# Gate/up of a pair ahead of the down product of the pair before it, in a two-layer decoder kernel with 64 experts

## What is computed

```python
def swiglu(x, wg, wu, wd):
    return (jax.nn.silu(x @ wg) * (x @ wu)) @ wd
top_idx, top_w = route(xf, w_router, router_bias)      # 8 of 64 experts for a token
y = routed_experts(xf, top_idx, top_w, w_gate, w_up, w_down) + swiglu(xf, ws_gate, ws_up, ws_down)
```

## Time and profile before

| | |
|---|---|
| median of 3 runs | 1187.65 us (1187.37 to 1188.17) |
| the profiled execution | 1188.19 us, its span 1186.4 us |
| mean granted clock of TensorE | 0.996 |
| PE busy | 1148.7 us (97%) |
| PEld, DVE, ACT busy | 523.0, 352.7, 255.3 us |
| HBM read, written | 452.22 MB, 3.15 MB; mean of all traffic 385 GB/s |
| the chain that ended last | PE 76%, DMA 21%, DVE 2% |

### The profile page before, as it was taken

The page is one execution under the profiler, slowest core; times in us unless marked ns, Lnnn a source line. Parts: engine busy times, 40 slices in busy tenths (PEclk is TensorE's granted clock), DMA queues, the critical chain, the costliest instruction groups (busy, mean ns, idle before and its releaser), DMA issues.

```text
span 1186.4 us, 15935 instructions
## 1 busy us (share of the span) xinstructions
PE 1148.7 (97%) x6752; PEld 523.0 (44%) x6752; DVE 352.7 (30%) x1053; ACT 255.3 (22%) x511; POOL 8.4 (1%) x20
## 2 busy tenths in 40 slices
PE   8999999999999999999999999999999999999995
PEld 7774633433343333333386655333343334333331
DVE  0424722222222222222333346232222222222224
ACT  1132421222122211111112323221222122112111
POOL 0000000000000000000000000000000000000001
PEclk9999999999999999999999999999999999999998
DMA  9982599999999999999998626999999999999995
GB/s 378 421 328 113 213 415 425 428 427 426 428 426 427 428 427 428 427 427 428 413 425 360 252 80 254 412 428 428 426 429 426 428 427 426 429 426 428 426 425 224
DMA packets 39952, 456.49 MB, mean 385 GB/s; under 512 B 4416, under 2 KB 4544, under 8 KB 8256
## 3 DMA queue, kind: packets, MB, share of 16 engines
q1 hardware_dynamic: 39872, 455.38, 91.5%
HBM read 452.22 MB, written 3.15 MB: 384 GB/s over the span
## 4 chain that ended last, share of the span: by engine, by line
PE 76%; DMA 21%; DVE 2%; issue 0%; ACT 0%; POOL 0%; POOLq 0%; DVEq 0%
PE bank L705 29%; DMA slots<-in_w_gu 20%; PE bank L725 14%; PE bank L926 5%; PE bank L854 5%; PE bank L607 4%; PE bank L634 4%; PE bank L863 2%; PE bank L1052 2%; PE bank L825 1%; PE bank L713 1%; PE bank L829 1%; PE bank L873 1%; PE bank L883 1%; PE bank L959 1%; PE bank L619 1%
## 5 line engine op out<-in xcount | busy, mean ns | idle before, releaser
L705 PE MATMUL bank<-slots,front 128*64 128x512 f32 x2048 | 456.0, 595 | 13.6 <-DMA slots<-in_w_gu 13.5
L705 PEld LDWEIGHTS bank<-slots,front 128*64 128x64 f32 x2048 | 139.9, 137 | 280.8 <-issue 249.4
L725 PE MATMUL bank<-slots,r 128*32 128x512 f32 x2016 | 229.9, 595 | 1.1 <-issue 1.1
L1403 DVE SCALAR_TENSOR_TENSOR yparts<-bank,small,yparts 128x512 fp32r<-128x512 f32 x128 | 96.0, 750 | 265.4 <-ACT yparts L1086 265.4
L1086 ACT ACTIVATE yparts<-bank,small 128x512 fp32r<-128x512 f32 x128 | 87.9, 687 | 239.8 <-PE bank L725 239.8
L1395 DVE TENSOR_TENSOR high<-high,bank 128x256 f32<-128x256 f32 x64 | 26.9, 421 | 354.5 <-ACT high L1113 326.7
L725 PEld LDWEIGHTS bank<-slots,r 128*32 128x32 f32 x2016 | 59.3, 109 | 137.2 <-issue 135.7
L1113 ACT ACTIVATE high<-bank 128x256 f32<-128x256 f32 x60 | 23.0, 384 | 413.1 <-PE bank L705 413.1
L1086 ACT ACTIVATE front<-bank 128x512 f32<-128x512 f32 (+1 forms) x161 | 84.5, 580 | 88.7 <-PE bank L825 28.2
L607 PEld LDWEIGHTS bank<-selr,xparts 128*128 128x128 f32 x512 | 64.3, 188 | 45.4 <-issue 45.4
L634 PE MATMUL bank<-yparts 64*128 64x512 f32 x512 | 79.4, 421 | 1.9 <-DVE yparts L1403 1.9
(11 more groups left out here) (123 smaller groups left out, 616.6 us busy)
## 6 DMA issues: line engine op xcount, KB each, us to landing
slots<-in_w_gu SPq DMA_DIRECT2D x116, 2048.0 KB, 30.8
slots<-in_w_dn SPq DMA_DIRECT2D x58, 2048.0 KB, 27.5
slots<-in_dense SPq DMA_DIRECT2D x28, 1024.0 KB, 14.8
slots<-in_w_gu SPq DMA_DIRECT2D x24, 1024.0 KB, 9.0
slots<-in_w_dn SPq DMA_DIRECT2D x10, 1024.0 KB, 37.4
slots<-in_first SPq DMA_DIRECT2D x3, 768.0 KB, 7.0
r<-in_pool_mat SPq DMA_DIRECT2D x2, 1024.0 KB, 25.9
sdn<-in_shared_dn SPq DMA_DIRECT2D x2, 1024.0 KB, 10.0
```

The source lines that it names most:

```text
L705: m = pe.matmul(H[64 * a:64 * a + 64, :], cells[:, cell(B, k, j), a, :], GU[g][:, a, :, k, :], start=k == 0, stop=k == KD - 1)
L725: m = pe.matmul(Y[half][r0:r0 + 32, :], hT[:, kc * P + 64 * a + 32 * t:kc * P + 64 * a + 32 * t + 32], wd[:, a, kc, :], start=kc == 0, sto ...
L1403: dve.scalar_tensor_tensor(ysp[:, 1, half * 512:(half + 1) * 512], Y[half][:, :], wslot[:, b:b + 1], ysp[:, 0, half * 512:(half + 1) * 512 ...
```

## The change

The first matmul group of body q is unchanged; what follows is reordered on all engines, in the main pass and in the spare passes (which run only if an expert has more than 32 tokens):

- PE, body q > 0: gate/up(q), both halves of down(q-1) (`down_both`), turn(q), gather, combine(q-1) half 0, gather, combine(q-1) half 1, turn_sel(q+1). Body 0 has no down. The body now covers all 32 pairs; pair 31's down comes behind the loop, with combine(30) half 1 between its halves, as before. At a block's first pair gate/up starts with six of eight gathers evacuated and waits for the others at k = 6 and 7.
- ACT: silu(q), both `hi` of q-1, then the two gathers' evacuations. DVE: `gated(q)`, `lo(q-1)` half 0, `turned(q)`, `lo(q-1)` half 1, `take_selT(q+1)`.
- SP: body q issues gate/up of q, then down of q-1.
- Pair 2's second gate/up half is loaded as two quarters. The first waits only for the first half of the shared expert's last product (`sgu_rd`) and is issued ahead of the load into `xs`, the second for `sh1` as before, behind it.

```diff
@@ SP
+                def give_dn(q):
+                    sp.wait_ge(ps.y_full, 2 * (base + q - 2))
...
+                        load_dn(ps, l, q, q % 3)
...
-                    sp.wait_ge(ps.y_full, 2 * (n - 2))
-                    load_dn(ps, l, q, g)
+                    if q > 3:
+                        give_dn(q - 1)
...
-                sp.wait_ge(*full_at(l, "sh1"))
-                load_gu(main, l, 2, 2, (1,))
+                a, m, z = W_CHUNK, W_CHUNK + W_CHUNK // 2, 2 * W_CHUNK
+                sp.wait_ge(sgu_rd, l + 1)
+                sp.dma_start(slots[:, 2, a:m], w_gu[l * PAIRS + 2][:, a:m]).then_inc(third_in, 16)
...
+                sp.wait_ge(*full_at(l, "sh1"))
+                sp.dma_start(slots[:, 2, m:z], w_gu[l * PAIRS + 2][:, m:z]).then_inc(main.w_in[1][2], 16)
@@ PE, body
                     gate_up(n, q, g, use, first)
+                    if first:
+                        refill(0)
+                        refill(1)
+                        if round_ is None:
+                            shared_turn(l, 1)
+                        turn_h(n)
+                    else:
+                        down_both(n - 1, q - 1, (q - 1) % 3, (q - 1) // 3)
+                        turn_h(n)
+                        begins = l if q == 1 and round_ is None else None
+                        if filling:
+                            refill(0)
+                        combine(ps, n - 1, 1 - b, 0, begins)
+                        if filling:
+                            refill(1)
+                        if not last:
+                            combine(ps, n - 1, 1 - b, 1, begins)
@@ PE, down_both
+                    pe.wait_ge(ps.hT_sb, n + 1)
...
+                        if B + 1 < BLOCKS:
+                            pe.wait_ge(ps.g_sb, first_fill + KD * (B + 1) + 2 * j + half + 1)
+                        else:
                             pe.wait_ge(ps.lo_rd, 2 * n - 1 + half)
                         down(q, g, half)
+                        if half == 0 and q == PAIRS - 1:
+                            combine(ps, n - 1, 0, 1)
@@ ACT, body
+                    if not first:
+                        hi(n - 1, 1 - b)
+                    if B + 1 < BLOCKS:
+                        for i in range(2):
+                            g_out(B + 1, 2 * j + i, Y[i])
@@ DVE, body
                     gated(n)
+                    if not first:
+                        lo(n - 1, 1 - b, 0, q == 1)
                     turned(n)
-                    for half in range(2):
-                        lo(n, b, half)
+                        lo(n - 1, 1 - b, 1)
                     if not last:
                         take_selT(n + 1, 1 - b)
```

More of the change, by code:

```diff
@@ L388, in pairs_of_pass @@
         def pairs_of_pass(base, body, start=0, ahead=None):
-            for q in range(start, PAIRS if ahead is None else PAIRS - 2):
+            for q in range(start, PAIRS):
                 body(base + q, q, q % 3, q % 2, q // 3, q == 0, q == PAIRS - 1)
@@ L690, in gate_up @@
                     B, j = q // SPAN, q % SPAN
+                    if j == 0 and B:
+                        pe.wait_ge(ps.g_sb, first_fill + KD * B + KD - 2)
                     if not first:
@@ L727, in down, with down_both @@
                     m.then_inc(ps.y_full, 1)
+                def down_both(n, q, g, use):
+                    pe.wait_ge(ps.hT_sb, n + 1)
+                    B, j = q // SPAN, q % SPAN
+                    main_last = round_ is None and q >= PAIRS - 2
+                    if round_ is None and q == SPLIT:
+                        pe.wait_ge(ahead_in, 16 * l + 16)
+                    for half in range(2):
+                        if main_last and half == 0:
+                            pe.wait_ge(half_in[q - PAIRS + 2], 16 * l + 16)
+                        else:
+                            pe.wait_ge(ps.w_in[2][g], (turn * USES[g] + use) * 16 + 16)
+                        if B + 1 < BLOCKS:
+                            pe.wait_ge(ps.g_sb, first_fill + KD * (B + 1) + 2 * j + half + 1)
+                        else:
+                            pe.wait_ge(ps.lo_rd, 2 * n - 1 + half)
+                        down(q, g, half)
+                        if half == 0 and q == PAIRS - 1:
+                            combine(ps, n - 1, 0, 1)
                 def body(n, q, g, b, use, first, last):
@@ L746, in body, with refill @@
[L746 to L749, removed]
+                    def refill(i):
+                        if i == 0 and j == 0:
+                            pe.wait_ge(ps.sel_rd, first_block + B + 2)
+                        if not first:
+                            pe.wait_ge(ps.lo_rd, 2 * n - 1 + i)
+                        gather(ps, 2 * j + i, Y[i])
+                    gate_up(n, q, g, use, first)
@@ L1055, in shared_up @@
                         filled(l, f"sh{t}", m)
+                    elif t == 1:
+                        m.then_inc(sgu_rd, 1)
                 turn_tile(0)
@@ L1109, in run @@
                     g_out(0, k, bank[FIRST_BANKS[k] if round_ is None else 4 + k % 4])
-                def body(n, q, g, b, use, first, last):
-                    act.wait_ge(ps.h_full, n + 1)
-                    act.activation(sg[:, 0, :], H[:, 0:F], ACT.Silu).then_inc(ps.silu_rd, 1)
-                    B, j = q // SPAN, q % SPAN
-                    if B + 1 < BLOCKS:
-                        for i in range(2):
-                            g_out(B + 1, 2 * j + i, Y[i])
-                    if first and round_ is None:
-                        shared_turned(l, 1)
-                    hi(n, b)
                 def hi(n, b):
@@ L1383, in body @@
                     gated(n)
+                    if not first:
+                        lo(n - 1, 1 - b, 0, q == 1)
                     turned(n)
-                    dve.wait_ge(ps.selT_sb, n + 1)
                     if not first:
-                        dve.wait_ge(ps.lo_rd, 2 * n)
-                    for half in range(2):
-                        lo(n, b, half)
+                        lo(n - 1, 1 - b, 1)
                     if not last:
@@ L1399, in turned, with lo @@
                     dve.tensor_copy(hT[:, 0:F], H[:, 0:F]).then_inc(ps.hT_sb, 1)
-                def lo(n, b, half):
+                def lo(n, b, half, first=False):
+                    if half == 0:
+                        dve.wait_ge(ps.selT_sb, n + 1)
+                        if not first:
+                            dve.wait_ge(ps.lo_rd, 2 * n)
                     dve.wait_ge(ps.hi_rd, 2 * n + half + 1)
```

106 lines of the change are left out of this document (24 added, 82 removed).

## The result

| | before | after |
|---|---|---|
| median of the runs | 1187.51 us (1187.06 to 1188.17, 4 runs) | 1194.93 us (1193.97 to 1195.91, 4 runs) |
| the profiled execution | 1188.19 us, span 1186.4 | 1195.31 us, span 1193.5 |
| PE busy | 1148.7 us (97%) | 1166.4 us (98%) |
| chain that ended last | PE 76%, DMA 21% | PE 96%, DMA 0% |

The changed kernel is **slower**: ratio 1.0062, 95% interval 1.0049 to 1.0075, +7.4 us by the medians. The forecast was 1186.4 with 1184.4 to 1190.6, so the measurement lies outside the range, on the side of the slower rival.

A forecast was written before the change was run, and what follows sets the result against it. PE and the loads were taken to run nearly level, with PE binding after the change. Down 30 earlier by 0.82 us in layer 0 and 0.39 in layer 1 gave -1.2 us, 1186.4, range 1184.4 to 1190.6.

The forecast's parts named there:

- slower rival: On PE, a gather between two combines drains it at each change: with 0.12 us more a pair, 1192.9 us; chance 0.25.
- Then 0.53 + 0.66 + 0.11: End of a PE pair, in us: second gather, combine half 1 and turn_sel, completing a pair of 13.54.
- the 5.25 wait: On PE, the second gather cannot start until 5.25 us after down starts, as DVE's `lo` half 1 must read Y[1].
- 577.06: Forecast start of down 30 in layer 0 on PE, in us, against 577.88 before: -0.82.
- -1.2 + 54 x (p - 13.54): Change of the total in us if a PE pair with gathers takes p: zero at 13.56, slower by over 0.2% from 13.61.
- price of 0.12: Cost in us of leaving a combine on PE, counted once a pair, for the lone combine behind the 5.25 wait.
- 2.45 - 1.45: Load stream per layer, in us: quarter moved into the DMA's idle stretch gains 2.45, a new hole behind it costs 1.45.
- 1.2 - 0.5 - 0.7: Load stream per layer, in us: hole at 176 goes (1.2), loads behind gate/up 2 and 3 come late (0.5, 0.7).
- The new hole at 150: DMA idle from about 150.2 until the load issued at 150.25 moves bytes at 151.4 to 151.9; taken as 1.45 us.
- the hole at 176: DMA low at 176 us in the kernel before, about 1.2 us; was to go, as gate/up 4 is released before down.
- the loads bind: Rival: a pair takes 13.50 or less and the last weight wait stays, -1.0 to -1.5 us a layer, 1184.9; chance 0.22.
- What was costed at nothing: Priced at zero: ACT's later evacuations, DVE's `build_sel` beside gate/up, SP's later down loads, layer 1's first load at 567.6.

The follow-up runs named there:

- e6_switches_in_before: The kernel before, its order of gate/up and down untouched, with combine half 0 put between the two gathers of a pair: 1188.79 us, ratio 1.0012.

## Why the prediction was wrong

**The step that failed** is in the sum for a pair, "Then 0.53 + 0.66 + 0.11": the lone gather behind the 5.25 wait was priced as half of two gathers that stand side by side and run on into the turn, all three of full height. Alone between two combines it measured 0.68. By the prediction's steps:

| step | predicted | measured |
|---|---|---|
| gate/up | 6.99 | 6.99 |
| down to second gather (floor) | 5.25 | 5.25 |
| of it waiting for `lo` | 0.05 | 0.10 |
| the lone gather | 0.53 | **0.68** |
| combine half 1 | 0.66 | 0.67 |
| turn_sel | 0.11 | 0.10 |
| a pair with gathers | 13.54 | 13.69 |
| start of gate/up 1, layer 0 | 157.54 | 157.32 |
| body 30, down 29 to down 30 | 13.01 | 13.02 |
| PE's waits for weights | near 0 | 0 |

0.15 a pair over 27 pairs is 4.1 us a layer: 577.06 + 4.1 - 0.2 = 581.0 against 581.27 measured, and over both layers 8.1 us, against the 8.5 between forecast (1186.4) and measurement (1194.9). The wait is 0.10 and not 0.05, as turn and first gather take 0.26 + 0.65 = 0.91 where 0.44 + 0.53 = 0.97 was taken; the floor of 5.25 hides that. The 0.3 left in layer 0 are rounding and small terms: the pairs without shared down average 13.70, those with it take 15.69 in place of 13.69 + 1.98, and the bodies 28 and 29 take 15.03 and 15.04 in place of 14.99.

One reading beside the sum was off as well, without moving it: the prediction took the listed 7.0 us for all that PE lost to weights, where the starts show 9.1. The new order had more to spend than it counted, and spent more still.

The **slower rival** was the right one, mechanism, place and formula: -1.2 + 54 x (p - 13.54) gives, for the p of 13.69 that was measured, +6.9, 1194.6 us. I gave it a price of 0.12 (that of leaving a combine) and a chance of 0.25. What was wrong is the weighing. The price stood in my own sum on one side only: I counted it for the lone combine and not for the lone gather beside it, although each has a change before and behind it. "Against: today's gathers already follow another mode at 1.06 for two" was the argument that misled: that row shows gathers entered by a change of tiling once and left without one. The Trainium skill (TensorEngine Tiling (Array Packing), Key Properties) says that a change of tiling mode drains TensorE. The runs agree in that a change costs time, 0.17 us each in `e6_switches_in_before`; what TensorE does in that time they don't show. Nor was the forecast robust: it lay 0.02 us a pair from no gain at all and 0.07 from "slower", and a range that ended at p = 13.62 cut off the rival's own central value of 13.66.

**The loads.** The sum was near, +1.0 us a layer forecast and 0.32 MiB = 0.8 us measured, but its parts were not: the quarters 2.45 - 1.45 = +1.0 forecast, and about -0.1 measured beside the new order (-0.7 us in layer 0 beside the old one); the order of release 1.2 - 0.5 - 0.7 = 0 forecast, and +0.9 measured. The new hole at 150 was foreseen; what was not is that the rates stay low behind it (the stretch from 152 to 156 us moves 348 GB/s with the quarters alone, 418 before, and that from 162 to 168 us 295 to 360 against 418 to 422), and that the hole at 176 comes back with the quarters. Together these eat the rest; why the rates are low is open. The prediction's "the loads bind" is what happens if the new order is used for eight pairs only, at 1 us of gain in the trace. None of this moved the total of the changed kernel, where TensorE binds.

**What was costed at nothing** and held: ACT's later evacuations and DVE's `build_sel` have no wait of PE beside them. Layer 1's first load went out at 571.95, not at 567.6, later by TensorE's own delay, and the chain shows no DMA behind it.

## What to carry to other kernels

Price an operation of TensorE by what stands before and behind it, from start to start: the same gather was 0.50 us in a row of eight, 0.53 in a pair, 0.68 alone. When a reorder interleaves operations of different tiles, count the changes of tiling in the loop body before and after (here four and six) and multiply by the passes. Where two resources run level, the waits of one are a budget, and it is read from the distances between starts rather than from the list of waits: 12.5 us in layer 0 were spent here against 9.1 us lost to weights (7.0 by the list), while eight pairs of the new order stayed within it.

## What was not expected of the hardware

- A change between operations of full and of half height costs about 0.17 us: 0.34 for two, shown by the same instructions in another order (13.59 against 13.25 us a pair).
- turn_sel (two transposes and two small matmuls in bf16, 128\*64 tiles) costs 0.10 behind a combine and ahead of gate/up, which has its tiling, but 0.36 between the turn and a gather (128\*128): 0.62 against 0.26 from turn to gather. With two changes more in its new place, the 0.26 on top are about 0.13 a change, an estimate from these two traces.
- A wait for weights that the profile lists at 1.15 us makes the pair 1.44 us longer from start to start (14.69 against 13.25).
- One load of 2 MiB issued as two of 1 MiB, the second behind another load, made the kernel slower by a ratio of 1.0020 (1.0011 to 1.0029) although the first went out no later (143.93 against 144.26); cause open.
